# A decoder layer on one core: all token tiles normed and turned first, then heads outside and tiles inside, with the projections and the retention gate as three rounded products each

## The reference

```python
mod = jax.nn.silu(c) @ w_ada + b_ada
sh1, sc1, g1, sh2, sc2, g2 = [m[:, None, :] for m in jnp.split(mod, 6, axis=-1)]
h = _rmsnorm(x, n1) * (1 + sc1) + sh1
rq, rk, rv, rg, sq, sk, sv, za, zb = _split_in(h @ w_in)
...
o_ret, ret_state = _retention(rq, rk, rv, ret_s0, ret_chunk)
o_ret = o_ret * lax.rsqrt(jnp.mean(o_ret * o_ret, axis=-1, keepdims=True) + NORM_EPS)
y_ret = (o_ret.reshape(B, T, -1).astype(x.dtype) * jax.nn.silu(rg)) @ w_up_ret
...
o_swa, k_buf, v_buf = swa_core(sq, sk, sv)
y_swa = o_swa @ w_up_swa
merged = jax.nn.sigmoid(za) * y_ret + jax.nn.sigmoid(zb) * y_swa
x = x + g1 * (merged @ w_o)
...
x = x + g2 * _apply_moe(h2, ...)
```

## Time and profile before

| | |
|---|---|
| time, median of 3 runs | 1430.8 us (1429.35 to 1432.86) |
| the profiled execution | 1428.8 us, span 1426.9 us |
| TensorE busy | 1284.2 us, 90% of the span |
| VectorE, ScalarE, GpSimd busy | 745.2, 479.5, 187.2 us |
| mixing stage (first projection to the last one's end) | 52.85 to 472.73 us |
| sample attention and gate | 482.87 to 561.87 us |

### The profile page before, as it was taken

One profiled execution on the slowest core, in us unless ns is written; L12 is line 12 of the kernel. 1 busy time (PEld: TensorE's weight loads), 2 busy tenths in 40 slices (PEclk: granted clock), 3 DMA queues, 4 the chain that ended last, 5 costly groups with the idle time before them and its releaser, 6 DMA issues.

```text
span 1426.9 us, 17550 instructions
## 1 busy us (share of the span) xinstructions
PE 1284.2 (90%) x6398; PEld 877.1 (61%) x6398; DVE 745.2 (52%) x1366; ACT 479.5 (34%) x787; POOL 187.2 (13%) x171
## 2 busy tenths in 40 slices
PE   3699999999999899999999997997389999998956
PEld 0455555555554467888888886885257666666622
DVE  0355555555565544111111116444769888888828
ACT  0122232222322123111111103111168887878732
POOL 1000000000000000000000001110012366444201
PEclk9899999999999999999999998998589999999978
DMA  9822202210201222111101005212769999999644
GB/s 345 341 82 76 81 6 81 76 54 33 81 7 72 78 100 89 45 45 45 40 35 34 23 5 216 86 67 69 294 215 374 369 359 359 369 353 364 259 194 181
DMA packets 35455, 214.06 MB, mean 150 GB/s; under 512 B 6884, under 2 KB 9892, under 8 KB 21714
## 3 DMA queue, kind: packets, MB, share of 16 engines
q1 hardware_dynamic: 26418, 191.34, 35.5%
q0 software_dynamic: 7392, 17.63, 3.6%
q10 hardware_dynamic: 1608, 4.60, 0.9%
HBM read 196.59 MB, written 24.80 MB: 155 GB/s over the span
## 4 chain that ended last, share of the span: by engine, by line
PE 63%; issue 15%; DMA 11%; DVE 7%; ACT 2%; POOL 1%; POOLq 0%; DVEq 0%; SPq 0%; ACTq 0%
PE p L1608 12%; PE p L1770 10%; DMA R<-in_we 9%; PE p L1862 7%; PE p L1774 6%; PE psS L1797 4%; PE p L1707 4%; PE psS L1770 3%; PE p L1797 3%; PE psS L1881 2%; PE psS L1774 2%; DVE R_rounded L1426 1%; PE psS L1574 1%; ACT R_rounded L869 1%; PE p L1813 1%
## 5 line engine op out<-in xcount | busy, mean ns | idle before, releaser
L1608 PE MATMUL p<-R 128*128 128x512 f32 (+1 forms) x576 | 271.5, 601 | 2.0 <-ACT R L652 2.0
L1862 PE MATMUL p<-R_rounded 128*96 128x512 f32 x768 | 196.5, 408 | 18.9 <-DVE R_rounded L1437 18.7
L1862 PEld LDWEIGHTS p<-R_rounded 128*96 128x96 f32 x768 | 123.3, 167 | 77.6 <-issue 31.0
L1426 DVE TENSOR_TENSOR R_rounded<-R,R_rounded 128x2048 fp32r<-128x2048 f32 x64 | 146.1, 2284 | 37.9 <-ACT R_rounded L869 37.8
L1608 PEld LDWEIGHTS p<-R 128*128 128x128 f32 (+1 forms) x576 | 93.5, 179 | 102.9 <-issue 98.8
L1770 PE MATMUL p<-R_rounded 128*128 128x344 f32 x864 | 142.7, 323 | 1.7 <-issue 1.7
L1241 DVE TENSOR_TENSOR work<-p,work 128x344 f32<-128x344 f32 x36 | 18.6, 517 | 233.4 <-ACT work L805 233.0
L1770 PEld LDWEIGHTS p<-R_rounded 128*128 128x128 f32 x864 | 136.9, 188 | 4.4 <-issue 2.2
L869 ACT CAST R_rounded<-R 128x2048 fp32r<-128x2048 f32 x64 | 122.5, 1915 | 27.8 <-DMA R<-in_we 22.0
L1881 PE MATMUL psS<-R_rounded 128*96 128x512 f32 x384 | 98.0, 404 | 5.4 <-DVE R_rounded L1449 5.4
L586 POOL DMA_INDIRECT y_dram<-R,slotY x32 | 82.6, 2582 | 100.0 <-ACT R L898 92.3
(11 more groups left out here) (276 smaller groups left out, 1775.3 us busy)
## 6 DMA issues: line engine op xcount, KB each, us to landing
R<-in_we SPq DMA_DIRECT2D x32, 2048.0 KB, 18.5
R<-in_we SPq DMA_DIRECT2D x32, 1024.0 KB, 18.9
R<-in_w_ada SPq DMA_DIRECT2D x8, 2048.0 KB, 7.8
R<-in_x SPq DMA_DIRECT2D x18, 512.0 KB, 3.3
R<-in_w_ada SPq DMA_DIRECT2D x8, 1024.0 KB, 12.7
R<-in_w_qkv SPq DMA_DIRECT2D x4, 2048.0 KB, 15.5
R<-in_lift SPq DMA_DIRECT2D x8, 1024.0 KB, 5.0
R<-y_dram SPq DMA_DIRECT2D x8, 1024.0 KB, 12.4
```

The costliest lines, as they stand in the source:

```text
L1426: nc.vector.tensor_tensor(half(we_lo[slot], u), half(we[slot], u), half(h13, u), ALU.subtract).then_inc(s["w13_lo"], 1)
L1608: last = mm(pj_bank[h % 2][0:rows, :], hst[:, k, 0:rows], wqh[:, h, k, :], start=k == 0, stop=k == KD - 1)
L1862: last = mm(up_bank[slot][0:CAP, :], x[:, k, :], kcols(w, k), start=k == 0 and j == 0, stop=k == KD - 1 and j == 2)
```

## The change

First all nine tiles are normed and turned, in one phase. The rows of x are scaled by their rstd on ScalarE (`normed`), turned on TensorE (`h_turn`), and scaled and shifted on VectorE per partition (`h_make`: the modulation is turned on TensorE too, and its way over `mod_dram` is gone for the first two blocks); then ScalarE rounds (`h_round`), VectorE takes the remainder (`h_rest`), and TensorE makes keys and values (`kv`) as three rounded products. The first head's weights are rounded in four parts in tiles 3 to 6.

Then the loop is written out, heads outside and tiles inside: 36 steps, `STEPS[m]` = (head, tile), with tile 8 the sample tokens'. The order of the parts within a step is as it was. `w_hi` has one buffer: when the ninth tile of a head is projected, `head_round` and `head_rest` bring in the next head's weights (and at the last, the gate's), part by part. The squares of o are taken step by step (`o_square`), and `norm_o` normalises one head's o at tile 2 of the next. The keys and values of all tiles stay in `K_all` and `V_all`. These and S lie where `oretT` is written later, so the first `o_out` waits for S's store. The gate's products are three rounded ones. The split of h ahead of the merge falls away. Most other lines of the diff place buffers.

```diff
+STEPS = [(h, t) for h in range(H) for t in range(NT + 1)]
+XG = (0, 1, 2, 2, 2, 3, 3, 3, 3)
+ADA_AT = {(NT + 1) * (i // 2) + (2, 6)[i % 2]: i for i in range(NT)}
...
+            sp.wait_ge(s["ada_mm"], 1)
+            x_load(2)
+            x_load(3)
+            weights(0)
+            for t in range(4, NT + 1):
+                x_load(t)
+            ada_bias(0)
+            for t in range(2, NT + 1):
+                sp.wait_ge(s["k_r"], t - 1)
+                rope_load(t, t)
...
+            for m, (h, t) in enumerate(STEPS):
+                if m < 2:
+                    sp.wait_ge(s["k_r"], NT + m)
+                elif STEPS[m - 2][1] == NT:
+                    sp.wait_ge(s["srot"], STEPS[m - 2][0] + 1)
+                else:
+                    sp.wait_ge(s["rot"], NT * STEPS[m - 2][0] + STEPS[m - 2][1] + 1)
+                rope_load(NT + 1 + m, t)
+                if m - 2 in ADA_AT:
+                    i = ADA_AT[m - 2]
+                    ada_out(i)
...
+                if t == 1 and h > 0:
+                    sp.wait_ge(s["pj"], (NT + 1) * h)
+                    weights(h + 1)
+            sp.wait_ge(s["pj"], len(STEPS))
             sp.dma_start(st_all, A["state"]).then_inc(s["sst_in"], 16)
-            sp.wait_ge(s["spj"], H)
+            sp.wait_ge(s["ada_mm"], 1 + NT)
             sp.dma_start(kwin[0:P - 1], A["ck"][1:P]).then_inc(s["swin_c"], 16)
             sp.dma_start(vwin[0:P - 1], A["cv"][1:P]).then_inc(s["swin_c"], 16)
             sp.wait_ge(s["k_r"], NT + 1)
             sp.wait_ge(s["v_e"], NT + 1)
-            sp.dma_start(kwin[P - 1:P], krot[0:NS, :]).then_inc(s["swin_c"], 16)
-            sp.dma_start(vwin[P - 1:P], V2[0:NS, P:2 * P]).then_inc(s["swin_c"], 16)
+            sp.dma_start(kwin[P - 1:P], krot[0][0:NS, :]).then_inc(s["swin_c"], 16)
+            sp.dma_start(vwin[P - 1:P], v8).then_inc(s["swin_c"], 16)
+            sp.wait_ge(s["st_u"], H * NT)
+            sp.dma_start(O["st_p"], S.rearrange("p h e -> p (h e)")).then_inc(s["stp_st"], 16)
             sp.wait_ge(s["swin_c"], 64)
...
+            for t in range(NT + 1):
+                if t < NT:
+                    normed(t + 1)
+                h_round(t)
+                if t + 2 <= NT:
+                    square(t + 2)
+                if t >= 1:
+                    v_out(t - 1)
+                if t >= 3:
+                    k_out(t - 3)
+                if 3 <= t < 7:
+                    head_round(0, t - 3)
+            k_out(NT - 2)
+            v_out(NT)
...
+            def head_round(hh, part):
+                act.wait_ge(s[f"wq_in{hh % 2}"], 16 * (hh // 2 + 1))
+                if hh and part < 3:
+                    act.wait_ge(s["wq_free"], 3 * (hh - 1) + part + 1)
+                elif hh:
+                    act.wait_ge(s["pj"], (NT + 1) * hh)
+                cols = slice(part * D, (part + 1) * D)
+                nc.scalar.copy(w_hi[:, cols], w_raw[hh % 2][:, cols]).then_inc(s["wq_hi"], 1)
...
+            for m in range(1, len(STEPS) + 1):
+                h, t = STEPS[m - 1]
+                n = NT * h + t
+                conv = h + 1 if m < len(STEPS) and STEPS[m][1] == NT else None
+                if t < NT:
+                    v_kd(n, h, m - 1)
+                    if m == 1:
+                        k_out(NT - 1)
+                        act.wait_ge(s["cache_st"], 32)
+                    qk_out(n)
...
+                if conv:
+                    head_round(conv, 0)
+                if m >= 2 and STEPS[m - 2][1] < NT:
+                    h2, t2_ = STEPS[m - 2]
+                    probs_out(NT * h2 + t2_)
+                    o_square(NT * h2 + t2_, h2, t2_)
+                if conv:
+                    head_round(conv, 1)
+                if t < NT:
+                    exps(n)
+                if conv:
+                    head_round(conv, 2)
+                    head_round(conv, 3)
...
+            act.wait_ge(s["stp_st"], 16)
             for t in range(NT):
                 o_out(t)
...
+            def h_make(t):
+                if t:
+                    dve.wait_ge(s["h_lo"], t)
+                for j, b in enumerate(turn_bank[t % 2]):
+                    dve.wait_ge(s["hT_t"], 2 * t + j + 1)
+                    bk = b.rearrange("p (k t) -> p k t", k=4)
+                    if t < NT:
+                        for k in range(4):
+                            kk = 4 * j + k
+                            last = nc.vector.tensor_scalar(hst[:, kk, :], bk[:, k, :], A1T[:, kk, 0:1], B1T[:, kk, 0:1],
+                                                           ALU.mult, ALU.add)
...
+                last.then_inc(s["h_r"], 1)
+            def h_rest(t):
+                w = P if t < NT else NS
+                dve.wait_ge(s["h_hi"], t + 1)
+                nc.vector.tensor_tensor(hlo[:, :, t * P:t * P + w], hst[:, :, 0:w], hhi[:, :, t * P:t * P + w], ALU.subtract
+                                        ).then_inc(s["h_lo"], 1)
+            def head_rest(hh, part):
+                cols = slice(part * D, (part + 1) * D)
+                dve.wait_ge(s["wq_hi"], 4 * hh + part + 1)
+                nc.vector.tensor_tensor(w_lo[hh % 2][:, cols], w_raw[hh % 2][:, cols], w_hi[:, cols], ALU.subtract
+                                        ).then_inc(s["wq_lo"], 1)
...
+            def norm_o(h):
+                dve.wait_ge(s["or_r"], h + 1)
+                x = o_all[:, 0:NT, h * P:(h + 1) * P]
+                r = orstd[:, 0:H * NT].rearrange("p (t h o) -> p h t o", h=H, o=1)[:, h]
+                nc.vector.tensor_tensor(x, x, r.to_broadcast([P, NT, P]), ALU.mult).then_inc(s["on_r"], 1)
+            for m in range(1, len(STEPS) + 1):
+                h, t = STEPS[m - 1]
+                n = NT * h + t
+                conv = h + 1 if m < len(STEPS) and STEPS[m][1] == NT else None
+                if t < NT:
+                    rotation(n, m - 1)
+                else:
+                    rotation_s(h, m - 1)
+                if conv:
+                    head_rest(conv, 0)
+                if m >= 2 and STEPS[m - 2][1] < NT:
+                    h2, t2_ = STEPS[m - 2]
+                    normalise(NT * h2 + t2_)
+                    window_out(NT * h2 + t2_, h2, t2_)
+                if conv:
+                    head_rest(conv, 1)
+                if t < NT:
+                    weigh(n, h)
+                if conv:
+                    head_rest(conv, 2)
+                if m in ADA_AT:
...
+                if t < NT:
+                    retention_out(n, h, t)
+                if conv:
+                    head_rest(conv, 3)
+                if h > 0 and t == 2:
+                    norm_o(h - 1)
             dve.wait_ge(s["srot"], H)
             dve.wait_ge(s["sv_c"], H)
...
+            def products(out, rows, t0, w, hi, lo):
+                ks, done = w
                 for k in ks:
-                    last = mm(p6[:, 0:256], hst[:, k, :], wkv[:, k, :], start=k == 0, stop=k == KD - 1)
-                if k == KD - 1:
-                    last.then_inc(s["kv_mm"], 1)
-            pe.wait_ge(s["h_r"], 1)
+                    for j, (x, y) in enumerate(((hT_hi, hi), (hT_hi, lo), (hT_lo, hi))):
+                        last = mm(out, x[k][:, t0:t0 + rows], y(k), start=k == 0 and j == 0, stop=k == KD - 1 and j == 2)
+                if done:
+                    last.then_inc(s[done], 1)
+            def kv(t):
+                rows = P if t < NT else NS
+                pe.wait_ge(s["h_lo"], t + 1)
+                if t == 0:
+                    pe.wait_ge(s["kv_lo"], 1)
+                if t >= 2:
+                    pe.wait_ge(s["k_r"], t - 1)
+                    pe.wait_ge(s["v_e"], t - 1)
+                products(kv_bank[t % 2][0:rows, 0:256], rows, t * P, (range(KD), "kv_mm"),
+                         lambda k: kv_hi[:, k * 256:(k + 1) * 256], lambda k: kv_lo[:, k * 256:(k + 1) * 256])
...
+            ada_first(0)
             h_turn(0)
             h_turn(1)
-            pe.wait_ge(s["hT_e"], 2)
-            pe.wait_ge(s["wkv_in"], 16)
-            kv(range(KD))
+            ada_first(1)
+            pe.wait_ge(s["mod_r"], 1)
+            for q in range(4):
+                last = nc.tensor.transpose(p2[:, q * P:(q + 1) * P], mod[:, q * P:(q + 1) * P], ident)
+            last.then_inc(s["modT_t"], 1)
+            kv(0)
+            for t in range(2, NT + 1):
+                h_turn(t)
+                kv(t - 1)
+                if t >= 3:
+                    k_turn(t - 3)
+            kv(NT)
+            k_turn(NT - 2)
...
+            def project_h(m, part):
+                h, t = STEPS[m]
+                rows = P if t < NT else NS
+                if t == 0:
+                    pe.wait_ge(s["wq_lo"], 4 * h + part + 1)
+                if part == 0 and m >= 2 and STEPS[m - 2][1] == NT:
+                    pe.wait_ge(s["srot"], h)
+                    pe.wait_ge(s["sv_c"], h)
+                done = "pj" if part == 3 else "wq_free" if t == NT else None
```

(33 more changed lines are left out.)

738 lines of the change are left out of this document (317 added, 421 removed).

## The result

The kernel after takes **1485.6 us** (median of 4, 1484.47 to 1488.24), the one before 1431.6 on the same chip: 1.0388 times as long, 95% interval 1.0372 to 1.0404. The profiled execution took 1488.2 us (span 1486.0). TensorE is busy for less time than before, 1259.5 us, and for less of the span, 85%.

The account below looks back on a forecast made before the run. TensorE, busy 382.2 of 391 us, was taken to pace the mixing stage. 1428.8 + 47.6 (front) - 42.1 (loop) + 9.6 (clock) + 44.9 (tail) + 2.5 (low clock after it) - 8.0 (gate) = 1483.3 us; range 1465 to 1495.

Parts of the forecast that it names:

- Front: Before the loop: with all nine tiles first, head 0's first product moves from 52.85 to 100.4 us, +47.6.
- Plain step: One plain head step in the loop: only parts 3 and 4 give back time, 10.15 to 9.49 us.
- Switches: Three head switches: roundings and remainders delay normalising; a pair of steps takes 26.3 us, plus 3.2 for a lowered clock.
- The late rope row: In the loop: the first rope row arrives late, behind 4 MB of weights, costing 1.0 us.
- Tail: Last projection to first sample product: ScalarE's first `o_out` waits for S's store behind the cache rows; 10.1 becomes 55, +44.9.
- the store is not held up: Tail rival: S's store is served beside the cache rows or SP isn't blocked; 12 replaces 44.9 + 2.5, 1448; chance 0.18.
- Gate: Gate products before the merge: 24 rounded ones take 3.99 us against 4.69 for an fp32 set; -8.0 us in all.
- The loop runs at TensorE's own rate: Loop rival: VectorE's chain runs ahead, steps 8.83, pairs 15.6, no clock loss; 57.6 less, 1416 us; chance 0.05.
- The clock rival: Front and switches: clock stays down, TensorE sets the front's tile, +12, and switches cost 4.8 each; 1500 us; chance 0.14.

Follow-up runs that it names:

- fill run: Kernel after, with TensorE turning a constant into an unused bank in the head switches' holes (28 and 40 times): 1472.3 us.
- all edits: Kernel after, with new switch order, x before head weights, head remainders one tile later, S stored first on SyncE, cache loads split 112 and 15 rows: 1393.5 us.
- early store: Kernel after, with SyncE storing S as its first transfer behind the last projection, ahead of state and cache rows: 1455.7 us.

## Why the prediction was right, point by point

**The total** was forecast at 1483 and measured 1485.6. The five spans of the table came out within about 4 us each, not only their sum. Inside the loop, though, misses of 4 to 5 us cancelled, and there the closeness is luck.

**Front, +47.6, measured +51.1.** The wait for x in tile 2 is where it was put (51.3 forecast, 52.98 measured), and its cause is shown by the run with x first. The serial tile was sized at 6.8 and took 7.2: the chain is the forecast's, with 2.63 for scale and shift (8 operations at 71.51) where 1.7 was put.

**Plain step, 9.49, measured 9.30.** The fixed point is VectorE's chain, shown by the run with two products. The forecast put it at 3.76, where TensorE itself had got to before and waited for nothing, and not at 3.60, where VectorE's probabilities were there. Measured was 3.60: 24 x 0.19 = 4.6 us.

**Switches, 26.3 + 3.2 a pair, measured 30.1.** Both holes stand ahead of `turn_probs`, 3.8 and 5.1 for 4.2 and 6.1. With the holes filled a pair took 25.4, so the order costs 0.9 less than forecast, and the clock 4.7 instead of 3.2; these two misses cancel in part. The 3.2 was a weighting between 0 and 4.8, and in this execution both holes brought the clock down, which others with the same loop did not all do. The last sample step, which the forecast left without a clock term, took 14.7 instead of 12.3. By the medians the fill run puts the clock's whole share at 13.3 us, of which 9.6 was forecast.

**The late rope row, 1.0 us, is the term most off.** The first step t = 1 took 13.9 us, the three others 7.5. VectorE waited for that row until 114.58, behind 4 MB of weights; `turn_qk` began at 117.25, 4.55 us after TensorE's last product. Nothing was run on this, and the kernel with all edits still has it (12.5 us). It is about 5 us more than forecast, and cancels what the plain steps gave.

**Tail, 55 us, measured 54.6.** The size was right, the reason at most half shown. The forecast gave the whole delay to the store's share on the DMA engine of the cache rows: "the row shows that engine busy throughout". The run with the store in ScalarE's queue shows that a busy engine is not enough, since a store passes those rows in 5.8 us. Behind them in SP's queue the store did land with the rows, 47.8 us behind the last projection (49 forecast), but SP also stood blocked at two single-row transfers until 529.34. Which of the two holds the store stays open. The forecast had the issue times of 8.20 and 19.61 and counted them inside the engine's time, and either reason gives the same sum. The rival "the store is not held up" was priced at 12 in place of 47.4, 35 less; the early store gave 30 and ended at 23.5 us instead of 22.

**Gate, -8.0, measured -8.4** from the two traces alone.

**The other side.** "The loop runs at TensorE's own rate" was not so in the kernel as changed, but the run with another order on the two engines came close to its pairs (16.6 against 15.6). Its time, 1440.1, stayed above that rival's 1416, in part because the plain steps keep VectorE's wait (9.30 against 8.83, 11 us over 24 steps). The 1393.5 with all edits has the tail's and the front's edits too, which the rival did not have.

**The clock rival** was half right. Its 4.8 us a pair at the switches came (4.7). In the front the clock did fall in part (0.57 in 56 to 64, 0.91 over 64 to 104), but TensorE did not set the tile: it still waited 1.6 to 3.1 us for VectorE ahead of the kv products of tiles 4 to 7.
